# First layer: heads 4 to 7 queried for all four token tiles in the latent ranking, context columns made there, twelve early experts in the context ranking

## The reference, cut to what matters

```
q = (xt @ w_q).reshape(n, 8, 2, 128)
s = einsum('nhpd,hpkd->nhpk', q, keys)             # 128 keys on each of two sides
sv, si = top_k(s, 16)
cand = sv[:, :, 0, :, None] + sv[:, :, 1, None, :]
cs, ci = top_k(cand, 16);  eidx = the pair's expert number
gate = softmax(cs)
a = einsum('nd,nhkd->nhk', xt, u[eidx])
out = einsum('nhk,nhkd->nd', gate * gelu(a), v[eidx])
```

## Time and profile before

| | us |
|---|---|
| median of 3 runs | 3808.6 (3805.99 to 3814.3) |
| the profiled execution | 3813.3 |
| its span | 3811.5 |
| PE busy in the span | 3620.6 (95%) |
| DVE busy | 2698.6 (71%) |
| ACT busy | 1711.8 (45%) |
| POOL busy | 698.4 (18%) |

### The profile page before, as it was taken

One profiled execution on the slowest core, in us unless ns is written; L12 is line 12 of the kernel. 1 busy time (PEld: TensorE's weight loads), 2 busy tenths in 40 slices (PEclk: granted clock), 3 DMA queues, 4 the chain that ended last, 5 costly groups with the idle time before them and its releaser, 6 DMA issues. The chain is left out here.

```text
span 3811.5 us, 57545 instructions
## 1 busy us (share of the span) xinstructions
PE 3620.6 (95%) x21555; PEld 3183.0 (84%) x21555; DVE 2698.6 (71%) x5248; ACT 1711.8 (45%) x2741; POOL 698.4 (18%) x668
## 2 busy tenths in 40 slices
PE   8997999989999986999999999999978999999998
PEld 8875888877878866988999999999966998888887
DVE  5674656656554769897888758888566887777776
ACT  4454445445543544553232333232245554555554
POOL 0001000000010104574444313333010650000000
PEclk9998999999999998999999999999989999999999
DMA  7556656565542123357888858888422366555664
GB/s 268 184 210 236 227 187 219 186 237 197 187 146 95 55 80 122 122 210 293 304 314 297 322 185 321 303 309 308 177 95 69 126 267 230 210 213 218 215 217 165
DMA packets 166767, 793.59 MB, mean 208 GB/s; under 512 B 16897, under 2 KB 58465, under 8 KB 97281
## 3 DMA queue, kind: packets, MB, share of 16 engines
q1 hardware_dynamic: 120496, 603.89, 43.3%
q0 software_dynamic: 45744, 186.36, 13.7%
q10 hardware_dynamic: 288, 0.15, 0.0%
HBM read 740.41 MB, written 47.28 MB: 207 GB/s over the span
## 5 line engine op out<-in xcount | busy, mean ns | idle before, releaser
L247 DVE TENSOR_TENSOR units<-ring,units 128x1024 fp32r<-128x1024 f32 x869 | 1063.5, 1226 | 522.8 <-ACT units L240 522.0
L240 ACT ACTIVATE units<-ring 128x1024 fp32r<-128x1024 f32 x928 | 978.1, 1056 | 897.9 <-PE ps L277 746.0
L276 PE MATMUL ps<-units,weighted 128*128 128x512 f32 x1280 | 501.4, 392 | 0.0
L275 PE MATMUL ps<-units,weighted 128*128 128x512 f32 x1280 | 499.4, 390 | 1.1 <-DVE units L247 1.1
L277 PE MATMUL ps<-units,weighted 128*128 128x512 f32 x1280 | 500.3, 391 | 0.0
L275 PE MATMUL ps<-wide_four,units 128*128 128x384 f32 (+1 forms) x1240 | 405.4, 327 | 6.0 <-PEq L3755 4.9
L277 PE MATMUL ps<-wide_four,units 128*128 128x384 f32 (+1 forms) x1240 | 403.6, 325 | 0.0
L276 PE MATMUL ps<-wide_four,units 128*128 128x384 f32 (+1 forms) x1240 | 403.0, 325 | 0.0
L277 PEld LDWEIGHTS ps<-units,weighted 128*128 128x128 f32 x1280 | 240.3, 188 | 51.1
L275 PEld LDWEIGHTS ps<-units,weighted 128*128 128x128 f32 x1280 | 240.9, 188 | 46.1 <-DVE units L247 1.5
L276 PEld LDWEIGHTS ps<-units,weighted 128*128 128x128 f32 x1280 | 240.7, 188 | 43.6
(11 more groups left out here) (592 smaller groups left out, 7640.8 us busy)
## 6 DMA issues: line engine op xcount, KB each, us to landing
ring<-in_stream SPq DMA_DIRECT2D x469, 1024.0 KB, 4.9
quad_ring<-in_mod_w POOLq DMA_DIRECT2D x12, 4096.0 KB, 14.7
gates_dram<-gates_place SPq DMA_DIRECT2D x20, 2048.0 KB, 7.2
gates_place<-gates_dram SPq DMA_DIRECT2D x15, 1536.0 KB, 13.2
gates_place<-gates_dram SPq DMA_DIRECT2D x15, 1024.0 KB, 5.9
gain_rows<-in_norm_gains SPq DMA_DIRECT2D x6, 512.0 KB, 5.1
peer_keys<-in_keys SPq DMA_DIRECT2D x3, 1024.0 KB, 6.4
gates_place<-gates_place SPq DMA_DIRECT2D x20, 128.0 KB, 2.0
```

The costliest lines, as they stand in the source:

```text
L240: act.activation(K.parts(n)[0], K.raw(n), ACT.Copy).then_inc(K.sig("hi_made").sem, units_to(K, n))
L247: dve.tensor_tensor(lo, K.raw(n), hi.bitcast(FP32), ALU.subtract).then_inc(K.sig("unit_split").sem, units_to(K, n))
L275: pe.matmul(out, w[0], x[0], start=start, stop=False)
L276: pe.matmul(out, w[0], x[1], start=False, stop=False)
```

## The change

The first layer's two rankings share four heads.

- In the latent ranking, heads 0 to 3 are as before. Heads 4 to 7 are multiplied for all four token tiles at once: 48 matmuls of 512 columns, in full PSUM banks. ScalarE copies the latent half as queries, and behind the scores' copy the context half into `peer_q_kept`. The scores have two banks, not three.
- For that, the context columns are made in the latent ranking: the squares at step 0 on ScalarE, the root at step 1; mean, reciprocal and scaling of the rows on DVE at step 0, ahead of the first ranks; turning on PE two columns at a time ahead of the units of heads 2 and 3 (bank 6 in two halves); whole columns on ScalarE at steps 2 to 4; all parts on DVE at step 3, ahead of the ranks of head 3. PE waits for each column's low part at head 4.
- The context ranking has no head of its own any more. It starts with the scores of the four given heads (4 to 7), and then multiplies heads 0 to 3. Twelve early experts, not five, follow. Ten are copied out to their own place and two to another, and gelu runs over them in two instructions. The spreads of key numbers stand behind chosen early experts. GpSimd's `joined_first` add stands behind the last split.
- The stream repeats only four heads' weights for the context, and the unsplit units start 7 units later.

The diff, cut:

```diff
-AHEAD_BOTH = 5, 5, 3
+AHEAD_BOTH = 12, 5, 3
+SHARED = 4
+class PairedModulated(TiledModulated):
+    def bank(self, K, k):
+        return K.ps[:, self.banks[0], k % 2 * SEQ:(k % 2 + 1) * SEQ]
...
-            if step == 1:
+            if step == 0:
                 square_rows(self.K, act, self.following)
-            elif step == 3:
+            elif step == 1:
                 root_of_mean(self.K, act, self.following)
+    def columns_scalar(self, act, step, part):
+        at = {(SHARED - 2, 1): 0, (SHARED - 1, 0): 2, (SHARED - 1, 1): 4, (SHARED, 0): 6}.get((step, part))
+        if self.following is not None and at is not None:
+            whole_scalar(self.K, act, self.following, range(at, at + 2))
     def step_vector(self, dve, step):
         if self.following is not None:
-            if step == 2:
-                mean_of_squares(self.K, dve, self.following)
-            elif step == 4:
-                reciprocal_root(self.K, dve, self.following)
+            if step == 0:
+                prepare_vector(self.K, dve, self.following)
+            elif step == SHARED - 1:
+                parts_vector(self.K, dve, self.following, range(KD))
+    def turn_following(self, pe, c, half):
+        n = 2 * (c - SHARED + 2) + half
+        if self.following is not None and 0 <= n < 4:
+            if n:
+                pe.wait_ge(*self.following.read(2 * n))
+            turn_tensor(self.K, pe, self.following, range(2 * n, 2 * n + 2))
+    def wait_following(self, pe, k):
+        pe.wait_ge(*self.following.low_made.at(k + 1))
...
 class SecondRouteHead:
     def scalar(self, act):
-        whole_scalar(self.K, act, self.E)
+        pass
     def vector(self, dve):
-        scale_rows(self.K, dve, self.E)
-        parts_vector(self.K, dve, self.E, range(KD))
+        pass
     def tensor(self, pe):
         keep_awake(self.K, pe, 0, 14)
-        turn_tensor(self.K, pe, self.E)
...
+    given = 0 if ready is None else PEER_HEADS - SHARED
+    asked = PEER_HEADS - given
+    first_u = 2 * asked
+    heads = [(c + PEER_HEADS - given) % PEER_HEADS for c in range(PEER_HEADS)]
...
+        def queries(n):
+            return K.ps[:, n % 2 * 2:n % 2 * 2 + 2, 0:2 * SEQ if beside is not None and n >= SHARED else SEQ]
...
                     split_lo(K, pool, n0 + n)
-                    if n == first_u + 1 and whole is not None:
+                    if n == units - 1 and whole is not None:
+                        pool.wait_ge(*scored.at(PEER_HEADS))
                         out, hi, lo = whole
                         pool.tensor_tensor(out, hi, lo, ALU.add).then_inc(K.sig("columns_joined").sem, 1)
...
                 head.tensor(pe)
-                for c in range(PEER_HEADS):
+                for c in range(given):
+                    score(c)
+                for c in range(given, PEER_HEADS):
+                    n = c - given
+                    joint = beside is not None and c >= SHARED
+                    if joint and c >= SHARED + 2:
+                        pe.wait_ge(*K.sig("pair_copied").at(c - SHARED - 1))
                     for half in range(2):
+                        head.turn_following(pe, c, half)
                         wait_unit(K, pe, u)
...
+                                if joint and (c, m) == (SHARED, 0):
+                                    head.wait_following(pe, 4 * half + k)
-                                last = product3(pe, K.ps[:, c % 2 * 2 + m, 0:SEQ],
+                                last = product3(pe, queries(n)[:, m, :],
                                                 [p[:, k, m * P:(m + 1) * P] for p in weight],
-                                                [pair(h, 4 * half + k) for h in range(2)],
+                                                [(beside[0] if joint else pair)(h, 4 * half + k) for h in range(2)],
...
                 head.scalar(act)
+                for c in range(given):
+                    take_scores(c)
+                for step in range(asked + 1):
+                    n = step - 1
+                    c = given + n
+                    if n >= 0:
+                        act.wait_ge(unit_used, n0 + 2 * n + 2)
+                        act.activation(query(c), queries(n)[:, :, 0:SEQ], ACT.Copy).then_inc(q_ready.sem, 1)
+                        head.columns_scalar(act, step, 0)
+                    if step < asked:
                         split_hi(K, act, n0 + 2 * step + 2)
+                    if n >= 0:
+                        take_scores(c)
+                        if beside is not None and c >= SHARED:
+                            act.activation(beside[1][:, 2 * (c - SHARED):2 * (c - SHARED) + 2, :], queries(n)[:, :, SEQ:2 * SEQ], ACT.Copy)\
+                               .then_inc(K.sig("pair_copied").sem, 1)
+                    head.columns_scalar(act, step, 1)
+                    if step < asked:
                         split_hi(K, act, n0 + 2 * step + 3)
                     head.step_scalar(act, step)
...
+                after = {0: (1,), 2: (2,), 4: (3,), 7: (4,), 9: (5, 6, 7)} if given else {0: (6,), ahead - 4: (7,)}
                 for e in range(ahead - 2):
                     take_early(e)
                     if e < ahead - 3:
                         split_hi(K, act, n0 + first_u + 3 + e)
-                    if e == 0:
-                        spread_numbers(6)
-                    if e == ahead - 4:
-                        spread_numbers(7)
+                    for c in after.get(e, ()):
+                        spread_numbers(c)
...
+                        act.activation(gelued[:, 0:raw[0], :], gelued[:, 0:raw[0], :], ACT.Gelu)
+                        last = act.activation(gelued[:, raw[0]:ahead, :], raw[1], ACT.Gelu)
...
-    return [(0, a), (a, PEER_HEADS), (a, peer), (second, between), (second + between, peer)]
+    return [(0, a), (a, PEER_HEADS), (a, SHARED), (a + PEER_HEADS, peer - PEER_HEADS), (second, between), (second + between, peer)]
```

More of the change, by code:

```diff
@@ L572, in low_parts_gpsimd, with whole_scalar @@
                            ALU.subtract).then_inc(E.low_made.sem, 1)
-def whole_scalar(K, act, E):
-    for k in range(KD):
+def whole_scalar(K, act, E, columns=range(KD)):
+    for k in columns:
         act.wait_ge(*E.turned.at(k + 1))
@@ L839, in past @@
         self.E.past()
+        if self.following is not None:
+            self.following.past()
         for S in self.sums:
@@ L3363, in __init__, with route @@
         self.second = K.over("picked_second", [P, PICKED], top - 4 * (D + 3 * PICKED + 3 * P))
-def route(K, pair, moving, routes, keys_dram, hit_whole, head, lent, ahead=0, gelued=None, whole=None, picked=None):
+def route(K, pair, moving, routes, keys_dram, hit_whole, head, lent, ahead=0, gelued=None, whole=None, picked=None,
+          beside=None, ready=None, raw=None):
     HP = 2 * PEER_HEADS
@@ L3386, in route, with query @@
     with ExitStack() as local:
[L3387 to L3390, removed]
+        q_place, s_place = lent
+        own = q_place.rearrange("p (h n) -> p h n", n=SEQ)
+        s = s_place.rearrange("p (t h n) -> p t h n", t=MT, h=HP)
+        def query(c):
+            if c < given:
+                return ready[:, 2 * c:2 * c + 2, :]
+            at = 2 * ((c - given) % (own.shape[1] // 2))
+            return own[:, at:at + 2, :]
+        def queries(n):
+            return K.ps[:, n % 2 * 2:n % 2 * 2 + 2, 0:2 * SEQ if beside is not None and n >= SHARED else SEQ]
+        score_banks = 3 if beside is None else 2
         keys = K.sbuf("peer_keys", [P, HP, KEYS], ctx=local)
@@ L3414, in _ @@
                 head.sync(sp)
[L3415 removed]
+                stream_weights(K, sp, asked + ahead // 2)
                 head.sync_end(sp)
@@ L3535, in _ @@
                     if step == 2:
-                        act.wait_ge(*tables_made.at(1))
-                        act.activation(ident[:, :], K.ident[:, :], ACT.Copy)
-                        act.activation(ranks[:, :, :], iota[:, :].unsqueeze(2).broadcast_to([P, TOPK, CH]), ACT.Copy)\
-                           .then_inc(tables_made.sem, 1)
-                    if step >= 4:
+                        make_ranks()
+                    if step >= 4 and not given:
                         spread_numbers(step - 4)
@@ L3543, in _ @@
                     split_hi(K, act, n0 + first_u + 2)
-                spread_numbers(5)
+                if given:
+                    spread_numbers(0)
+                else:
+                    spread_numbers(5)
                 if picked is not None:
@@ L3660, in route @@
     head.past()
+    if beside is not None:
+        K.sig("pair_copied").past(PEER_HEADS - SHARED)
     if whole is not None:
@@ L4239, in second_block @@
               AHEAD_BOTH[0], early[:, 0:AHEAD_BOTH[0], :],
               [a.rearrange("p t k n -> p t (k n)") for a in (joined[:, :, :, :], four[:, 0:3, 0, :, :].bitcast(FP32),
-                                                             four[:, 0:3, 1, :, :].bitcast(FP32))], picked)
```

(2 more changed lines are left out.)

94 lines of the change are left out of this document (52 added, 42 removed).

## The result

The changed kernel takes 3822.8 us (median of 8 runs, 3818.6 to 3826.7), the kernel before 3810.4 us (8 runs, 3806.0 to 3814.3): a ratio of 1.0033, 95% interval 1.0022 to 1.0044. The profiled execution took 3826.3 us, its span is 3824.5: 13.0 us more than before. It is 0.3% slower, within the range and for most of the reasons given.

A forecast was written before the change was run, and what follows sets the result against it. DVE bounds the latent ranking's end, PE the experts' main stretch. Latent ranking +28.5, context ranking +10.0 and experts -29.5 sum to +9.0 us: median 3817.5 us from 3808.6, range 3803 to 3825.

The forecast's parts named there:

- The wide heads and what stands ahead of head 4: Latent ranking: wide matmuls and PE's delays before them bring last scores 35.5 us late; less 7.0 hidden, 28.5 longer.
- (b): Latent ranking: DVE scales the context rows late, behind the root and a GpSimd hold, so PE waits 2.5 us.
- (c): Latent ranking: PE turns later column pairs only after ScalarE made the pair before; stops of 0.6, 2.0 and 0.6 us.
- (e): Latent ranking, ahead of head 4: PE waits for DVE's low parts of context columns, with a GpSimd hold, 5.7 us.
- (d): Latent ranking: 16 transposes of context columns on PE at 0.16 us each, 2.6 us.
- (a): Latent ranking: ScalarE's two squares move to step 0, ahead of head 0's query copy, costing PE 0.7 us.
- The lag: End of the latent ranking: DVE starts ranking head 7 7.0 us behind its scores, hiding that much of PE's delay.
- Context ranking: First layer's context stage: late exponential costs 7.8 us, joining add's hold 2.7, start gains 0.5; 10.0 longer, 102 us.
- Experts: Main loop: seven experts leave it, saving their activations on PE, 7 x 4.22 = 29.5 us less.
- Rival C: Longer stretch of expert outputs starves; with each of seven new ones 1 us longer, 3824.5 us; chance 0.10.
- A: Rival: PE is fed without stops; latent stage grows only 16.4 us, context stage by PE's 5.5: 3801 us; chance 0.12.
- B: Rival: GpSimd's holds of DVE are absent or fall elsewhere; +1.7 us, 3810, no change that can be told; chance 0.23.

The follow-up runs named there:

- the earlier pairs: On top of the four edits, ScalarE makes two context column pairs and takes the root earlier, without idle transposes ahead of head 2: 3811.7 us, ratio 0.9996.
- the four edits: Changed kernel with joining add early, exponential first, PE turning the identity during key loading and ahead of head 2, low parts in two steps: 3808.0 us, ratio 0.9992.
- the last run: On top of the four edits, the first layer's keys are loaded once, with 14 identity turns ahead of the given heads' scores: 3804.1 us, ratio 0.9983.

## Why the prediction was right, and where not

**The wide heads and what stands ahead of head 4** (+28.5, stage 124): 124.2. Copies of the wide heads' queries are 11.81 us apart (11.8 predicted), the last scores were copied at 1532.75. (b) was 2.3 us for 2.5; in (c) the stops were 0.45, 1.88 and 0.45 for 0.6, 2.0 and 0.6; (e) is a stop of 5.7 as predicted, and the low parts in two steps took the stage down by 5.8. That the total agrees is partly luck. The low clock behind the stops was left out: 3.0 us, by the run that kept PE busy. Against it stand (d), 16 transposes at 0.10 us instead of 0.16 and so 0.9 short, (a), 0.5 at PE for 0.7, and 8.1 us that were hidden, not 7.0 (last scores' copy to the end 26.6 us, before 34.7). The lag itself was 7.1. The other 1.0 is from head 7's rank to the end of the stage, 26.0 us where the kernel before takes 27.0. The prediction had called that part unchanged, its low clock too, and named a change there as a sign of being wrong: PE rested 16.9 us ahead of it and no longer 23.9, and fewer of its transposes ran slow.

**Context ranking** (+10.0, stage 102): 105.8 in that execution, 103.5 and 103.7 in two others with the same code there. The mechanism is shown by the runs with the early add, the early exponential and both: 2.6 us by the one, nothing by the other alone, and about 1.1 more by it once the add is gone. What is over is the clock again: the 32 scores of the given heads took 6.5 us where 0.93 a head was counted (3.7), and 2.8 of the 3.4 us are this; the other 0.6 lie at PE's end, where the clock was 0.86 from 1653 us on. The scores take 5.0 to 5.2 in the other executions that stop for the keys, and 3.5 to 3.6 where PE was kept busy. That term, four given heads, was sized at the full clock though PE had stood 3.2 us for the keys, and the earlier trace rows had shown that it falls when PE rests.

**Experts** (-29.5): -29.4, and 29.5 come back with five early experts. Rival C is refuted: PE is busy in 750 of 750 us.

**The step that failed** is "Not changed: spreading the routes, the second layer." The add's move was in the diff, in a function of three callers; I priced it for one. It is 3.2 us by the rows, and moving it back there alone undoes just this. That the total still fell within the range, 13.0 us for 9.0, owes something to luck: the attention's unexplained -2.4 stands against these 3.2.

**Rivals.** A (PE fed without stops, 3801) is the direction of the later runs: with the stops shortened the kernel gets to 3808, 0.08% below the kernel before where A had 0.2%, since in the latent ranking DVE becomes the bound (the earlier pairs). B (no holds) is refuted by the product's 1.21, 3.84 and 6.94 us. Open is why the second layer's attention took 164.1 us here, 163.9 to 165.8 in the other kernels with twelve early experts and 166.5 in both with five; no experiment was aimed at it.

What the change does for the time is then plain. It takes 29.5 us of PE's work from a stretch where PE is the bound and puts it where PE had rested; that cost 28.3 and 11 to 13 in place of nothing, because PE's rest was behind DVE's work and the new work had to come ahead of it. With the places in the engines' orders mended it costs 21.7 to 24.1 (the four edits, and the last run) and 6.1.

## What to carry to other kernels

When a diff moves a line in a shared function, price the line once for every caller. Work given to an idle engine is free only where its inputs exist before the rest begins; otherwise it buys a stop at each place where another engine's order has them late, and a stop of PE can cost twice, once as time and once as low clock behind it. When two waits cover one end, test them together too: here one alone showed nothing. And before a difference of 2 us between two profiled executions is given to an edit, look at what the same code does in another execution.

## What the runs showed of the hardware

- The granted clock falls in short stops, and not each time. Behind the 2.3 us of stops ahead of head 2, 17 or 18 products started 0.21 us apart in the changed kernel and in the four other runs that leave this part as it is; with the low parts in two steps, whose stops there were the same, they were 0.12 apart. Behind the 2.2 us stop in head 4 eight were 0.43 apart in the last run (clock 1.00 up to the stop's end, then 0.53) and 0.23 with all four edits. Two executions of the same code differed by 2.1 to 2.4 us in a stage, nearly all by that. Turning the identity while PE waits (46 transposes in 5.2 us) took it away where it was placed right.
- GpSimd's instruction holds a bf16 product of DVE as whole as a float32 one: 1.21 us became 3.84 and 6.94, in both cases up to 1.1 us behind the add's end. The sum ahead of it (0.42 us, one input) was not held. One input alone does not keep an instruction free, though: the float32 to fp32r conversion of 256 columns, one input in SBUF, took 2.52 us instead of 0.29 beside a split of GpSimd, in the run with the earlier pairs.
